# Experts' tokens gathered two pairs at a time, by fp32r products of 256 columns

## What is computed

```
t = 256; xt = rms_norm(x)                      # 256 x 1024
g_sel = argmax(xt @ w_group + b_group)         # one of 4 groups
e_logit = (xt @ w_expert + b_expert)[group]    # 8 experts of that group
top_p, top_i = top_k(softmax(e_logit), 2)      # two experts a token
gate = g_w * top_p / sum(top_p)
for each expert e:                             # 32 experts
    rows = xt[tokens of e]
    y = (silu(rows @ w1[e]) * (rows @ w3[e])) @ w2[e]   # 1024 -> 512 -> 1024
    out[tokens of e] += gate * y
return rms_norm(x + out) * g_final
```

## Time and profile before

| what | value |
|---|---|
| median of 3 runs | 1363.15 us (1363.07 to 1370.86) |
| the profiled execution's own time | 1361.37 us |
| its span | 1359.6 us |
| TensorE busy | 1285.8 us, 95% of the span |
| VectorE, ScalarE, GpSimd busy | 510.5, 549.0, 568.2 us |
| bytes moved by DMA | 341.22 MB, 251 GB/s on average |

### The profile page before, as it was taken

How to read it: one execution, slowest core, us unless ns; L and a number is a source line. 1 busy time by engine, 2 the same in 40 slices (tenths; PEclk the granted TensorE clock), 3 DMA queues, 4 the chain that set the end, 5 groups by cost and what they waited for, 6 DMA issues and landing times.

```text
span 1359.6 us, 20047 instructions
## 1 busy us (share of the span) xinstructions
PE 1285.8 (95%) x7971; PEld 958.3 (70%) x7971; DVE 510.5 (38%) x1307; ACT 549.0 (40%) x853; POOL 568.2 (42%) x132
## 2 busy tenths in 40 slices
PE   6999999999998899999999899999999999999996
PEld 5867899998986799999877788854445444454442
DVE  2334544445265454444657264431112111121113
ACT  4544655556477465555544465221111111111112
POOL 5532788885954188888568555400000000000000
PEclk9999999999999999999999899999999999999998
DMA  7622566654633176665446443599999999999994
GB/s 268 216 81 89 154 199 200 190 187 154 217 124 94 62 213 190 186 185 172 154 147 201 135 145 128 208 422 426 429 429 428 428 428 430 429 430 429 429 427 176
DMA packets 154821, 341.22 MB, mean 251 GB/s; under 512 B 8473, under 2 KB 119418, under 8 KB 142202
## 3 DMA queue, kind: packets, MB, share of 16 engines
q1 hardware_dynamic: 154746, 340.18, 67.2%
HBM read 339.10 MB, written 1.05 MB: 250 GB/s over the span
## 4 chain that ended last, share of the span: by engine, by line
PE 72%; DMA 15%; DVE 5%; ACT 4%; POOL 2%; issue 2%; SPq 0%; ACTq 0%; DVEq 0%
PE bank L649 16%; PE bank L651 15%; PE bank L650 15%; DMA ring<-in_w 10%; PE bank L1211 10%; PE bank L1237 5%; DMA xspare<-in_w 4%; PE bank L1163 2%; PE bank L748 2%; POOL parts L611 2%; PE bank L659 1%; ACT parts L1281 1%; PE bank L1193 1%; PE bank L1097 1%; PE bank L782 1%
## 5 line engine op out<-in xcount | busy, mean ns | idle before, releaser
L611 POOL TENSOR_TENSOR parts<-raw,parts 128x2048 fp32r<-128x2048 f32 (+4 forms) x128 | 568.0, 4465 | 305.5 <-ACT parts L1281 305.5
L649 PE MATMUL bank<-xh,parts 128*128 128x256 f32 x1032 | 289.0, 280 | 12.1 <-ACT room L1318 5.9
L650 PE MATMUL bank<-xl,parts 128*128 128x256 f32 x1032 | 286.7, 278 | 0.0
L651 PE MATMUL bank<-xh,parts 128*128 128x256 f32 x1032 | 286.6, 278 | 0.0
L1281 ACT ACTIVATE parts<-raw 128x2048 fp32r<-128x2048 f32 (+4 forms) x128 | 235.9, 1853 | 33.1 <-PE bank L649 18.0
L1211 PE MATMUL bank<-ring,room 128*64 128x512 f32 x768 | 226.2, 594 | 8.6 <-DMA ring<-in_w 5.8
L649 PEld LDWEIGHTS bank<-xh,parts 128*128 128x128 f32 x1032 | 194.5, 189 | 18.9 <-issue 10.6
L650 PEld LDWEIGHTS bank<-xl,parts 128*128 128x128 f32 x1032 | 195.3, 189 | 0.8
L651 PEld LDWEIGHTS bank<-xh,parts 128*128 128x128 f32 x1032 | 194.6, 189 | 0.0
L1211 PEld LDWEIGHTS bank<-ring,room 128*64 128x64 f32 x768 | 73.3, 137 | 112.5 <-issue 112.5
L649 PE MATMUL bank<-parts,xh 128*128 128x512 f32 (+5 forms) x304 | 114.6, 377 | 9.6 <-POOL parts L611 2.8
(11 more groups left out here) (255 smaller groups left out, 1804.4 us busy)
## 6 DMA issues: line engine op xcount, KB each, us to landing
ring<-in_w SPq DMA_DIRECT2D x71, 2048.0 KB, 23.1
raw<-in_ffn_w_up SPq DMA_DIRECT2D x88, 512.0 KB, 4.9
room<-in_w SPq DMA_DIRECT2D x12, 2048.0 KB, 20.1
raw<-in_ffn_w_down SPq DMA_DIRECT2D x44, 512.0 KB, 3.9
xspare<-in_w SPq DMA_DIRECT2D x11, 2048.0 KB, 26.8
raw<-in_w_in SPq DMA_DIRECT2D x40, 512.0 KB, 4.2
raw<-in_diff_w_qkv SPq DMA_DIRECT2D x24, 512.0 KB, 4.5
raw<-in_mla_w_o SPq DMA_DIRECT2D x8, 512.0 KB, 4.6
```

Source lines behind the costliest of these rows:

```text
L611: pool.tensor_tensor(low[:, p % PARTS, 0:n], raw[:, p % RING, 0:n], high[:, p % PARTS, 0:n], ALU.subtract).then_inc(low_ready, 1)
L649: first = pe.matmul(out_, a[0], b[0], start=start, stop=False)
L650: pe.matmul(out_, a[0], b[1], start=False, stop=False)
L651: return first, pe.matmul(out_, a[1], b[0], start=False, stop=stop)
```

## The change

The rows of `xn` are no longer scaled in place and multiplied in float32. ScalarE writes their scaled high part as fp32r (`row_high`, in place of tables and gains that nobody needs any more), and VectorE the low part (`rows_r`: the scaled row less its high part). A gather now serves two pairs at once: `Sel` has the columns of four experts, 256 in all, and each block of 128 features is four fp32r products (high and low part, two blocks of tokens) in place of two float32 products of 128 columns for each pair. Half of the eight blocks of features is done beside one pair, half beside the other, for the two pairs that follow. So there are two `XgT` and two `Sel`, used in turn. The last two pairs gather nothing. Before the first pair both halves are gathered.

```diff
-        XgT = r3(view(0, KT * P), b=P)
-        hid = view(1024, EF)
...
+        XgT = [r3(view(2 * KT * P * b, 2 * KT * P), b=2 * P) for b in range(2)]
+        hid = view(4096, EF)
...
+        Sel = [y.rearrange("p (t e c) -> p t e c", t=NT, e=4) for y in (
+            room_r[:, 5632:5632 + NT * 4 * CAP], score_r[:, :, :].rearrange("p a b -> p (a b)"))]
+        row_high = [gains_r[:, :], tables_r[:, C_DIST:C_DIST + D]]
...
-            pe.wait_ge(rows_scaled, NT)
+            pe.wait_ge(rows_split, NT)
-            def gather(n, first=0, last=KT, frees=0):
-                if first == 0:
-                    pe.wait_ge(sel_ready, 1 + n)
+            def gather(half, at, first, last, sel, b=2, frees=0):
                 for k in range(first, last):
-                    for t in range(NT):
-                        ins = pe.matmul(bank[2 + k // 4][:, P * (k % 4):P * (k % 4) + P],
-                                        xn[:, t, P * k:P * k + P], Sel[:, t].rearrange("p e c -> p (e c)"),
-                                        start=t == 0, stop=t == NT - 1)
...
+                    for x in range(2):
+                        for t in range(NT):
+                            row = (row_high[t], rows_r[:, t, :])[x][:, P * (at + k):P * (at + k) + P]
+                            ins = pe.matmul(bank[b + k // 2][:, 2 * P * (k % 2):2 * P * (k % 2) + 2 * P], row,
+                                            Sel[sel][:, t].rearrange("p e c -> p (e c)"),
+                                            start=x == 0 and t == 0, stop=x == 1 and t == NT - 1)
...
-                if not last:
-                    gather(n + 1, 0, 6, frees=1)
+                if gathers:
+                    pe.wait_ge(sel_ready, (4 if j % 2 == 0 else 3) + n)
+                    gather(n + 2, 4 * (j % 2), 0, 2, (j // 2 + 1) % 2, frees=1)
                 pe.wait_ge(hidden_ready, 1 + n)
...
-                if not last:
-                    gather(n + 1, 6, KT)
-                    pe.wait_ge(xg_ready, 3 + 2 * n)
+                if gathers:
+                    pe.wait_ge(selT_ready, 1 + n)
+                    gather(n + 2, 4 * (j % 2), 2, 4, (j // 2 + 1) % 2)
+                    pe.wait_ge(xg_ready, 5 + 2 * n)
...
-                gather(base)
+                pe.wait_ge(sel_ready, 2 + base)
+                gather(base, 0, 0, 4, 0)
+                gather(base + 1, 4, 0, 4, 0, b=4)
...
-                act.activation(xn[:, t, :], xn[:, t, :], ACT.Copy, scale=st[:, 16 + t:17 + t]).then_inc(rows_scaled, 1)
+                act.activation(row_high[t], xn[:, t, :], ACT.Copy, scale=st[:, 16 + t:17 + t]).then_inc(rows_high, 1)
...
             dve.tensor_scalar(r_minus[:, 2:4], top_of[:, :, 0], -1.0, None, ALU.mult).then_inc(maxima, 1)
+            for t in range(NT):
+                dve.wait_ge(rows_high, t + 1)
+                dve.scalar_tensor_tensor(rows_r[:, t, :], xn[:, t, :], st[:, 16 + t:17 + t],
+                                         row_high[t], ALU.mult, ALU.subtract).then_inc(rows_split, 1)
             dve.wait_ge(mask_ready, 1)
```

More of the change, by code:

```diff
@@ L240, in build @@
         ring = sb("ring", [P, 3 * RING, HALF])
+        with nc.sbuf_tensor("tables_r", [P, C_END], F32R) as tables_r:
+            pass
         cs = sb("cs", [P, C_END])
@@ L244, in build @@
         convT = sb("convT", [P, 2, 4, 2, FT])
[L245 removed]
+        with nc.sbuf_tensor("gains_r", [P, D], F32R) as gains_r:
+            pass
+        gpre = sb("gpre", [P, D])
+        gpost = sb("gpost", [P, D])
         wr = sb("wr", [P, KT, NG + NE])
@@ L249, in build @@
         h = sb("h", [P, NT, D])
+        with nc.sbuf_tensor("rows_r", [P, NT, D], F32R) as rows_r:
+            pass
         xn = sb("xn", [P, NT, D])
@@ L257, in build @@
         att = sb("att", [P, 4, 2, 2, 2])
+        with nc.sbuf_tensor("room_r", [P, 11648], F32R) as room_r:
+            pass
         room = sb("room", [P, 11648])
@@ L298, in build @@
         qiT, kiT = qrT, krT
+        with nc.sbuf_tensor("score_r", [P, NT, S], F32R) as score_r:
+            pass
         score = sb("score", [P, NT, S])
@@ L1196, in scatter, with pair @@
                         ins.then_inc(moe_full, 1)
-            def pair(n, j, four, first=False, opens=False, last=False, start=False, by_halves=False):
-                pe.wait_ge(xg_ready, 1 + 2 * n)
+            def pair(n, j, four, first=False, opens=False, last=False, gathers=True, start=False, by_halves=False):
+                pe.wait_ge(xg_ready, 2 + 2 * n)
                 for x, done in enumerate((h1_full, h3_full)):
@@ L1256, in one_round @@
                     i = NP // TURN_PAIRS - 1
-                    pair(base + (TURN_PAIRS * i + j), j, fours + i, last=j == TURN_PAIRS - 1,
+                    pair(base + (TURN_PAIRS * i + j), j, fours + i, last=j == TURN_PAIRS - 1, gathers=j < 2,
                          by_halves=first and j == TURN_PAIRS - 1)
@@ L2219, in pair @@
                                          ALU.mult).then_inc(hidden_ready, 1)
-                if not last:
-                    take(n + 1)
+                if gathers:
+                    take(n + 2, j % 2, (j // 2 + 1) % 2)
                 for hf in range(2):
@@ L2234, in one_round @@
             def one_round(base):
-                with dve.Fori(0, NP // 2 - 1) as i:
-                    for odd in range(2):
-                        pair(base + 2 * i + odd, 2 * i + odd, odd)
-                pair(base + (NP - 2), NP - 2, 0)
-                pair(base + (NP - 1), NP - 1, 1, last=True)
-            select(0, 0, gates=False)
+                with dve.Fori(0, NP // 4 - 1) as i:
+                    for j in range(4):
+                        pair(base + 4 * i + j, 4 * i + j, j)
+                for j in range(4):
+                    pair(base + (NP - 4 + j), NP - 4 + j, j, gathers=j < 2, last=j == 3)
+            select(0, 0)
             dve.wait_ge(logits_exp, 4)
@@ L2251, in _ @@
             link(ins)
-            link(dve.tensor_copy(gpair, gate[:, :, 0:2]))
-            take(0)
+            gates_of(0).then_inc(gates_put, 1)
+            for half in range(2):
+                take(half, half, 0, 2 + 2 * half)
             dve.wait_ge(flag_ready, 1)
@@ L2262, in _ @@
                     dve.wait_ge(last_added, 4 * r)
-                    select(r * NP, 0)
-                    take(r * NP)
+                    select(0, 0)
+                    gates_of(0).then_inc(gates_put, 1)
+                    for half in range(2):
+                        take(r * NP + half, half, 0, 2 + 2 * half)
                     one_round(r * NP)
```

68 lines of the change are left out of this document (35 added, 33 removed).

## The result

The changed kernel took 1367.36 us (median of 20 runs) against 1362.55 of the kernel before (20 runs beside it): ratio 1.0037, 95% interval 1.0021 to 1.0053. The forecast was no change within 1%, at 1364.6 us, and that class came. The size did not: the forecast added 1.5 us, the medians differ by 4.8. The profiled executions are 1366.51 and 1361.37 us, 5.1 apart, with spans of 1364.7 and 1359.6 us.

The account below looks back on a forecast made before the run. The weight stream was taken as the bound: its start, 201 MB at its rate, plus standstills. 1361.4 us plus 1.5 (split 1.2, selections 0.3) gave 1362.9; the median's 1.8 above the profiled execution made it 1364.6, range 1361.5 to 1368.5.

Parts of the forecast that it names:

- Which resource sets the end: Experts: the weight stream at 428 GB/s, 29.4 us a pair, sets the end, not TensorE.
- TensorE's saving: Each expert pair: fp32r gathers shorten TensorE's pair from 27.7 to 26.2 us, hidden by the weight stream; worth 0 at the end.
- A delay of the first h1 arrives whole at the end: First pair: no reserve at the first issue after eight transfers, so the stream stands still as much longer, +1.5 us.
- Size of the split and of the selections: VectorE ahead of the first gather: splits delay posm by 1.2 us, wider selections add 0.3 us.
- rival 2: Clock falls before the first gather after TensorE's 3.0 us wait, 1.7 us more before first h1 is done: 1366.3; chance 0.22.
- the last pair: Last expert pair: only here would a clock fall at the waits for w1 be passed on, at most 1.5 us.
- the tail: From the last pair's h3 to the span's end: fixed at 29.6 us, as before.
- the waits for weights: TensorE in the experts: waits for data grow up to 2.8 us, some 30 us in all.
- rival 5: Experts: clock stays down for most of a pair after 2.8 us waits, making TensorE the bound; slower by over 1%; chance 0.03.
- Less than full speed in the experts: Sign of being wrong: the clock row showing less than full speed in the experts.
- Cases 1 to 3: The forecast (0.6), clock fall before the first gather (0.22), delay costing nothing (0.1): together 1363.1 to 1366.3 us.
- the split's bounds: VectorE ahead of the first gather: splits delay posm by 0 to 3.1 us, so −1.2 and +1.9 around the forecast.

Follow-up runs that it names:

- e7: Changed kernel loading half of every expert weight's bytes and multiplying with that half twice, so it computes something else; median 1337.05 us.
- e6: Kernel before, loading half of every expert weight's bytes and multiplying with that half twice, so it computes something else; median 1352.74 us.
- e1: Changed kernel with 11 unused TensorE products in the wait before the first gather; ratio 1.0022 to the kernel before.
- e2: Kernel before with the two splits added on VectorE at the same place, into tiles nobody reads; ratio 1.0017 to the kernel before.
- e9: Changed kernel with 11 unused products before the first gather, 8 per pair from the fifth, 64 small VectorE instructions ahead of the jump; ratio 1.0027 to kernel before.
- e10: As e9, but GpSimd makes the low part, ScalarE scales then rounds, no fill before the first gather; ratio 1.0072 to the kernel before.
- e5: Changed kernel with unused products before the first gather and behind all pairs but the last, without VectorE's further-rounds block; ratio 1.0027 to the kernel before.
- e3: Changed kernel without VectorE's jumped-over block for further rounds; ratio 1.0009 to the kernel before.
- e4: Kernel before with VectorE's jumped-over block made as long as the change makes it; ratio 0.9990 to the kernel before.
- e8: e4 with 24 more small instructions in the jumped-over block, so the jump lands at 1166; ratio 1.0022 to the kernel before.

## Why the prediction was right, and where it was short

**Which resource sets the end: right.** The chain is on transfers from 1030.53 us (forecast 1020 to 1060), the rate is 428 GB/s, a pair takes 26.18 us where TensorE sets the pace (933.58 to 959.76, the next pair's h3; forecast 26.2), h3 to w2 2.8 (forecast 2.7). e7 against e6 shows that TensorE's saving is real, and worth 15.7 us as soon as the weights do not bind. With whole weights none of it reached the end, as the prediction said: in the profiles start, clock and jump account for the whole difference.

**A delay of the first h1 arrives whole at the end: right.** It is 3.0 and 3.1 us in the kernel after, 1.4 and 1.4 in e1, 2.6 and 2.6 in e2, 1.4 and 1.15 in e9, 7.0 and 7.45 in e10 (first h1 and last h3 against before). Only e5, whose fills delay a later release as well, has 1.4 and 2.9.

**Size of the split and of the selections: right.** Forecast 1.2 and 0.3 us, measured 1.08 and 0.27 by VectorE's rows, and e9, which has only these left, is 1.1 us longer.

**The step that failed: that the clock stays up before the first gather.** The prediction made it rival 2, at 0.22, with 1.7 us. It came, and cost 1.7 us in the gather. The wait was 2.76 us where 3.0 was forecast, nearer to the 2.68 that had left the clock at 1.00 than to the 3.11 that had not the earlier trace rows, and e2 lost the clock after 2.49 us. So the chance could not be set by a threshold between two waits. The kernel after shows that no such threshold exists in its own loop, where TensorE waits for w1 behind the same products with w2 each time:

```profile
1176.37 1.94 PE L1228 MATMUL bank<-ring,room 128*64 128x512 f32 x8 [2.65 <-DMA ring<-in_w]
1205.68 2.83 PE L1228 MATMUL bank<-ring,room 128*64 128x512 f32 x6 [2.49 <-DMA ring<-in_w]
```

```profile
1176.37:1179.37 3.00, 3.00 (x14) 1.23 (x16) 0.00 (x0) 0.00 (x0) 0.00 (x0) 1.00 1.03 437
1205.68:1208.68 3.00, 3.00 (x8) 1.09 (x10) 0.00 (x0) 0.00 (x0) 0.00 (x0) 0.50 1.00 426
```

The longer wait left the clock at 1.00, the shorter one was followed by 0.50. What decides between them stays open. In the last pair it is the same: TensorE waits 1.18 to 1.19 us and then 0.69 ahead of w2's products in the kernel before and in e6, the same program with smaller transfers; the clock stayed at 1.00 in the one and fell to 0.50 in the other.

**What the prediction did not have: the tail.** It took 29.6 us as fixed. VectorE's wait of 2.01 us behind the jump is 1.9 of it. e3 shows that the wait goes with the block, and e9 that it can be absent with the block in place (by the jump's place or by TensorE's fills, which no run tells apart); e4 and e8 show that neither the block's length nor the place where the jump lands is enough. In each of the three profiles with this wait (the kernel after, e1, e7) a transfer of 16 KB of instructions lands at most 0.3 us before VectorE goes on, at 1355.5 us in the kernel after; in the kernel before the like transfer lands at 1352.6 us, while VectorE is at work. That VectorE waits for its own code is argued from that, not shown. Which places of the jump cost this stays open.

**The clock further on.** The prediction named the last pair, at up to 1.5 us. It fell there in e1, e3, e6 and e7, at 1.7 us, and not in the profiled execution of the kernel after. In the middle the waits for weights reach 3.8 us, above the 2.8 of the forecast, and are 22.8 us in all, where some 30 were forecast. The clock falls behind four of them (those that end at 1057.90, 1117.68, 1205.68 and 1294.06 us) and is at 1.00 again within 7 us of each, so rival 5 did not come. The page's clock row shows it as an 8 in the 33rd slice. "Less than full speed in the experts" was one of the prediction's own signs of being wrong; it came, and it points at the step that failed.

In the middle such a fall costs nothing: from 940 to 1120 us, where two of them begin, the rate is 428 GB/s all the same.

So the sum for the profiled execution is 1.4 (VectorE ahead of the first gather, and its selections) + 1.7 (clock) + 1.9 (jump) = 5.0, against 5.1 measured. The median, 1367.36, lies in the range; it was the forecast's mechanism with rival 2 and an addition that nobody had named. That it still lies there is in part luck: with 1.7 for the clock and 1.9 for the jump the forecast's own 1364.6 becomes 1368.2, 0.3 us inside a range that allowed nothing for the tail. Nor does the range follow from the terms named for it: cases 1 to 3 with the split's bounds and 1.8 us on either side would give 1360.1 to 1370.0. Of all the versions with the change and whole weights none is faster than the kernel before.

## What to carry to other kernels

Where transfers set the pace, ask of a change only whether it moves the moment at which a place is first free: that microsecond arrives at the end, while 1.4 us saved on TensorE in each of 14 pairs turned into waiting. Before crediting a shorter computation, halve the transfers in both kernels: if the gain shows only there, the change belongs to another kernel or another stage. And an engine that becomes early also waits longer, and may lose its clock: look where work that counts follows such a wait, at the first gather and in the last pair, and fill the wait only where the engine really is waiting.

## What the runs showed of the hardware that was not expected

- The length of the wait before it did not tell whether the granted clock falls: in one execution of the kernel after it fell to 0.50 behind a wait of 2.49 us and stayed at 1.00 behind one of 2.65, after the same products. At the first gather it fell behind 2.76 us (2.49 in e2), 0.7 us after TensorE had begun again, and was back about 4 us after the gather began; 11 products in the wait kept it at 1.00 (e1).
- Behind a jump over code that is not run VectorE stood still for 2.01 us (1.92 in e1, 1.80 in e7), and not at all in e4 and e8, whose blocks are as long. With 64 small instructions ahead of it and TensorE's fills the wait was gone (e9).
- GpSimd's subtraction of 1024 columns (2.34 to 2.39 us) held up VectorE's operations with two inputs in on-chip memory, 8 and 32 columns wide, for as long as it ran (e10).
- A split of 1024 columns to fp32r took 1.28 us, just like the nearest float32 form in the earlier trace rows: the output's type cost nothing.
